# A gated transformer kernel on one core: the RWKV time mixing with 64-row products, an interleaved second tile level, centred values, and squares by token halves

## The reference, cut to what matters

```python
kk = kk / max(norm(kk), 1e-12)                     # heads of 64
k = k * (1 + (a - 1) * k_a)
# per head, state S (value x key), over tokens:
S_t = S_{t-1} diag(w_t) + (S_{t-1} a_t) b_t^T + v_t k_t^T ;  y_t = S_t r_t
mu = mean(y, over the head's 64); var = mean((y - mu)**2)
y = (y - mu) * rsqrt(var + GN_EPS) * gn_w + gn_b
y = y + sum(r * k * r_k) * v
return (y * g) @ w_o
```

## Time and profile before

| | us |
|---|---|
| median of 3 runs | 1428.78 |
| lowest and highest | 1426.89, 1428.99 |
| span of the profiled execution, first to last instruction | 1420.2 |
| PE busy | 1375.6 |
| DVE busy | 1049.1 |
| ACT busy | 733.2 |

### The profile page before, as it was taken

The page is one execution under the profiler, slowest core; times in us unless marked ns, Lnnn a source line. Parts: engine busy times, 40 slices in busy tenths (PEclk is TensorE's granted clock), DMA queues, the critical chain, the costliest instruction groups (busy, mean ns, idle before and its releaser), DMA issues.

```text
span 1420.2 us, 30753 instructions
## 1 busy us (share of the span) xinstructions
PE 1375.6 (97%) x11830; PEld 1310.7 (92%) x11830; DVE 1049.1 (74%) x1649; ACT 733.2 (52%) x1194; POOL 219.2 (15%) x232
## 2 busy tenths in 40 slices
PE   8999999999999999999999999999999999999997
PEld 6998899999988899999878888799999998999997
DVE  7988799987887889974787965777774556677743
ACT  4547555644556556664366442554444447544442
POOL 0000133310000223320000010113320000133300
PEclk9999999999999999999999999999999999999999
DMA  9874367797663547675322300346666433466661
GB/s 377 303 258 171 123 226 234 258 394 252 205 226 105 208 165 254 216 232 173 151 98 90 120 2 2 116 133 186 188 208 203 141 115 120 144 197 197 208 205 69
DMA packets 68434, 258.20 MB, mean 182 GB/s; under 512 B 7545, under 2 KB 9857, under 8 KB 67970
## 3 DMA queue, kind: packets, MB, share of 16 engines
q1 hardware_dynamic: 68354, 257.10, 54.2%
HBM read 256.01 MB, written 1.06 MB: 181 GB/s over the span
## 4 chain that ended last, share of the span: by engine, by line
PE 81%; DVE 11%; ACT 3%; issue 2%; DMA 2%; DVEq 0%; ACTq 0%
PE ps L740 21%; PE ps L742 20%; PE ps L741 20%; PE ps L757 3%; DVE lo L1919 2%; PE ps L701 2%; PE ps L703 1%; PE ps L702 1%; ACT hi L1370 1%; DMA modraw<-in_wmod 1%; DVE U L2508 1%; DMA modlast<-in_wmod 1%; DVE products L2506 1%; DVE modraw L1925 1%; PE ps L764 1%
## 5 line engine op out<-in xcount | busy, mean ns | idle before, releaser
L1919 DVE TENSOR_TENSOR lo<-raw,hi 128x1024 fp32r<-128x1024 f32 (+1 forms) x350 | 476.5, 1378 | 168.5 <-ACT hi L1370 167.8
L740 PE MATMUL ps<-OH,lo 128*128 128x256 f32 x1920 | 540.8, 282 | 6.2 <-DVE lo L1919 6.0
L742 PE MATMUL ps<-OH,hi 128*128 128x256 f32 x1920 | 534.8, 279 | 0.0
L741 PE MATMUL ps<-OL,hi 128*128 128x256 f32 x1920 | 534.8, 279 | 0.0
L1370 ACT ACTIVATE hi<-raw 128x1024 fp32r<-128x1024 f32 (+1 forms) x350 | 381.0, 1112 | 10.4 <-DMA raw<-in_w 6.1
L740 PEld LDWEIGHTS ps<-OH,lo 128*128 128x128 f32 x1920 | 362.0, 189 | 12.7 <-DVE lo L1919 9.9
L741 PEld LDWEIGHTS ps<-OL,hi 128*128 128x128 f32 x1920 | 362.4, 189 | 0.0
L742 PEld LDWEIGHTS ps<-OH,hi 128*128 128x128 f32 x1920 | 361.0, 188 | 0.0
L740 PE MATMUL ps<-GH,lo 128*128 128x256 f32 x704 | 196.3, 279 | 0.0
L742 PE MATMUL ps<-GH,hi 128*128 128x256 f32 x704 | 196.2, 279 | 0.0
L741 PE MATMUL ps<-GL,hi 128*128 128x256 f32 x704 | 196.2, 279 | 0.0
(11 more groups left out here) (389 smaller groups left out, 2059.5 us busy)
## 6 DMA issues: line engine op xcount, KB each, us to landing
raw<-in_w SPq DMA_DIRECT2D x288, 512.0 KB, 3.9
raw<-in_w SPq DMA_DIRECT2D x64, 704.0 KB, 5.3
modraw<-in_wmod SPq DMA_DIRECT2D x71, 512.0 KB, 5.2
modlate<-in_wmod SPq DMA_DIRECT2D x10, 512.0 KB, 4.0
modlast<-in_wmod SPq DMA_DIRECT2D x7, 512.0 KB, 4.5
modfirst_a<-in_wmod SPq DMA_DIRECT2D x4, 512.0 KB, 11.4
modfirst_b<-in_wmod SPq DMA_DIRECT2D x4, 512.0 KB, 12.1
l<-in_lora_in SPq DMA_DIRECT2D x1, 1536.0 KB, 6.2
```

Source lines behind the costliest of these rows:

```text
L740: pe.matmul(bank[:, 0:T], lo[:, r, w], oh[:, k0 + k], start=first, stop=False)
L741: pe.matmul(bank[:, 0:T], hi[:, r, w], ol[:, k0 + k], start=False, stop=False)
L742: ins = pe.matmul(bank[:, 0:T], hi[:, r, w], oh[:, k0 + k], start=False, stop=final)
L1919: dve.tensor_tensor(lo[:, s, 0:kt * P], raw[:, s, 0:kt * P], hi[:, s, 0:kt * P].bitcast(F32), ALU.subtract).then_inc(lo_made, 1)
```

## The change

It has four parts.

1. `z_part` and `u_part` do each product as two, one for tokens 0 to 63 and one for tokens 64 to 127 (`TOKEN_HALVES`), each with a stationary matrix of 128 x 64.
2. `second_level(x, t)` replaces `second_x` and `second_t`: the second tile's x products alternate with the first tile's t products, and the second tile's t products stand behind `z_part(0)`. ACT and DVE lists follow.
3. DVE makes `centre` = identity minus 1/64 within a head, over the place of the constant `bucket`. The 16 transposes of `V_` become ordinary float32 products with it, so that `VR` holds centred values. The four sums of `Yc` and the four subtractions are gone.
4. Squares go by `PAIRS` (tile, half of the channels): two of the four, and half of the sums, move ahead of `y_part(2)`. The table of the root is loaded earlier; the splits of two weight units stand before and behind the root.

```diff
         ident, ones, heads_ones = const("ident"), const("ones"), const("heads")
+        centre = const("bucket")
...
+        TOKEN_HALVES = slice(0, RN), slice(RN, P)
...
-                    ins = pe.transpose(PS[g % 4][:, q * P:(q + 1) * P], rw_src(g, q), ident)
+                    if g < 4:
+                        ins = pe.matmul(PS[g % 4][:, q * P:(q + 1) * P], rw_src(g, q), centre, start=True, stop=True)
+                    else:
+                        ins = pe.transpose(PS[g % 4][:, q * P:(q + 1) * P], rw_src(g, q), ident)
...
-            def second_x(tb):
-                pe.wait_ge(S("zeros_made"), 1)
-                pe.wait_ge(S("level_by_act"), 2 * tb + 5)
-                pe.wait_ge(S("level_by_dve"), tb + 3)
-                for n in range(RH * tb, RH * (tb + 1)):
-                    ins = pe.matmul(PS[2 * tb + (n % RH) // 8][RN:P, (n % 8) * RN:(n % 8 + 1) * RN], AT[0:RN, n, RN:P],
-                                    Tm[0:RN, n], start=True, stop=True)
-                ins.then_inc(S("level_done"), 1)
...
-            def second_t(tb):
-                pe.wait_ge(S("zeros_made"), 4)
...
-                for n in range(RH * tb, RH * (tb + 1)):
-                    ins = pe.matmul(PS[2 * tb + (n % RH) // 8][0:RN, (n % 8) * RN:(n % 8 + 1) * RN], X64[tb][RN:P, n % RH],
-                                    TT[RN:P, n, RN:P], start=True, stop=True)
-                ins.then_inc(S("level_done"), 1)
+            def second_x(n):
+                tb = n // RH
+                return pe.matmul(PS[2 * tb + (n % RH) // 8][RN:P, (n % 8) * RN:(n % 8 + 1) * RN], AT[0:RN, n, RN:P],
+                                 Tm[0:RN, n], start=True, stop=True)
...
+            def second_t(n):
...
+            def second_level(x, t):
+                if x is not None:
+                    pe.wait_ge(S("zeros_made"), 1)
+                    pe.wait_ge(S("level_by_act"), 2 * x + 5)
+                    pe.wait_ge(S("level_by_dve"), x + 3)
+                if t is not None:
+                    pe.wait_ge(S("zeros_made"), 4)
+                    pe.wait_ge(S("diag_placed"), 1)
+                    pe.wait_ge(S("level_by_act"), t + 8)
+                    pe.wait_ge(S("level_by_dve"), t + 6)
+                for n in range(RH):
+                    if x is not None:
+                        last_x = second_x(RH * x + n)
+                        if n == RH - 1:
+                            last_x.then_inc(S("level_done"), 1)
+                    if t is not None:
+                        last_t = second_t(RH * t + n)
+                        if n == RH - 1:
+                            last_t.then_inc(S("level_done"), 1)
...
-                        ins = pe.matmul(dst, apk[k % 2][:, b % 2, q, 0:P], v, start=True, stop=(tb == 0))
+                        for t in TOKEN_HALVES:
+                            ins = pe.matmul(dst[t], apk[k % 2][:, b % 2, q, t], v, start=True, stop=(tb == 0))
                         if tb:
-                            ins = pe.matmul(dst, AR[:, 4 * (b // 2) + q, 1, 0], SZ[:, head(b, q)], start=False, stop=True)
+                            for t in TOKEN_HALVES:
+                                ins = pe.matmul(dst[t], AR[:, 4 * (b // 2) + q, 1, 0, t], SZ[:, head(b, q)], start=False, stop=True)
...
-                        ins = pe.matmul(bank_of(k)[:, (4 * (b % 2) + q) * RN:(4 * (b % 2) + q + 1) * RN],
-                                        TT[:, RH * tb + 4 * b + q], Zs[k % 2][:, b % 2, q], start=True, stop=True)
+                        for t in TOKEN_HALVES:
+                            ins = pe.matmul(bank_of(k)[t, (4 * (b % 2) + q) * RN:(4 * (b % 2) + q + 1) * RN],
+                                            TT[:, RH * tb + 4 * b + q, t], Zs[k % 2][:, b % 2, q], start=True, stop=True)
...
-            second_x(0)
-            second_x(1)
+            second_level(0, None)
             pe.wait_ge(S("apb_made"), 2)
             half_gram(1)
-            second_t(0)
-            second_t(1)
+            second_level(1, 0)
             z_part(0)
+            second_level(None, 1)
...
+            def square_sums(k):
+                tb, g = PAIRS[k]
+                pe.wait_ge(S("gnsq_ready"), k + 1)
+                for c in range(2 * g, 2 * g + 4):
+                    ins = half_sums(PS[4][0:RH, tb * P:(tb + 1) * P], GQ[:, c, tb * P:(tb + 1) * P], c)
+                if k == 3:
+                    ins.then_inc(S("gnvar_done"), 1)
+            pe.wait_ge(S("bon_by_v"), 4)
+            square_sums(0)
+            square_sums(1)
             y_part(2)
             y_part(3)
-            pe.wait_ge(S("bon_by_v"), 4)
-            pe.wait_ge(S("yc_copied"), 4)
-            for g in range(4):
-                pe.matmul(PS[g][:, :], heads_ones, Yc[:, 2 * g:2 * g + 2].rearrange("p c t -> p (c t)"),
-                          start=True, stop=True).then_inc(S("gnsum_done"), 1)
-            for c in range(DC):
-                pe.wait_ge(S("gnsq_ready"), c // 2 + 1)
-                ins = half_sums(PS[4][0:RH, 0:T], GQ[:, c], c)
-            ins.then_inc(S("gnvar_done"), 1)
+            square_sums(2)
+            square_sums(3)
...
+            place_diagonal(3)
             for tb in range(2):
                 act.wait_ge(S("level_done"), tb + 5)
...
                 if tb == 0:
-                    place_diagonal(3)
-            place_diagonal(0)
-            place_diagonal(1)
+                    place_diagonal(0)
...
+            def square(k):
+                tb, g = PAIRS[k]
+                part = slice(2 * g, 2 * g + 4), slice(tb * P, (tb + 1) * P)
+                act.wait_ge(S("yc_copied"), k + 1)
+                act.activation(GQ[:, part[0], part[1]], Yc[:, part[0], part[1]], ACT.Square).then_inc(S("gnsq_ready"), 1)
+            square(0)
+            square(1)
+            act.preload_act_table(ACT.Sqrt)
             z_copy(3)
-            for copy in (u_copy, y_copy):
-                copy(2)
-                copy(3)
-            for r in range(LEAD, SLOTS):
-                weights_hi("rw_v", COUNT["rw_v"] // SLOTS - 1, r, KT)
-            act.preload_act_table(ACT.Sqrt)
-            for g in range(4):
-                act.wait_ge(S("gn_centred"), g + 1)
-                act.activation(GQ[:, 2 * g:2 * g + 2], Yc[:, 2 * g:2 * g + 2], ACT.Square).then_inc(S("gnsq_ready"), 1)
+            u_copy(2)
+            u_copy(3)
+            y_copy(2)
+            square(2)
+            y_copy(3)
+            square(3)
+            weights_hi("rw_v", COUNT["rw_v"] // SLOTS - 1, LEAD, KT)
             take_root(root[0:RH, 0], PS[4][0:RH, 0:T], 1 / RN, gn_eps[0:RH], S("gnvar_done"), 1, S("stage_root"))
+            weights_hi("rw_v", COUNT["rw_v"] // SLOTS - 1, LEAD + 1, KT)
...
+            chain.add(stt(out=centre, in0=heads_ones, scalar=-1 / RN, in1=ident, op0=ALU.mult, op1=ALU.add))
...
+            half_masks(1)
             second_x_out(1)
-            half_masks(1)
...
-            for g in range(4):
-                dve.wait_ge(S("gnsum_done"), g + 1)
-                y = Yc[:, 2 * g:2 * g + 2].rearrange("p c t -> p (c t)")
-                stt(out=y, in0=PS[g][:, :], scalar=-1 / RN, in1=y, op0=ALU.mult, op1=ALU.add).then_inc(S("gn_centred"), 1)
-            for r in range(LEAD, SLOTS):
-                weights_lo("rw_v", COUNT["rw_v"] // SLOTS - 1, r, KT)
             dve.wait_ge(S("g_scaled"), DC)
-            def by_gain(g):
-                dve.wait_ge(S("gnsq_ready"), g + 1)
-                chain.add(dve.tensor_tensor(Yc[:, 2 * g:2 * g + 2], Yc[:, 2 * g:2 * g + 2], G2[:, 2 * g:2 * g + 2], ALU.mult))
-            by_gain(0)
-            by_gain(1)
+            def by_gain(k):
+                tb, g = PAIRS[k]
+                part = slice(2 * g, 2 * g + 4), slice(tb * P, (tb + 1) * P)
+                dve.wait_ge(S("gnsq_ready"), k + 1)
+                chain.add(dve.tensor_tensor(Yc[:, part[0], part[1]], Yc[:, part[0], part[1]], G2[:, part[0], part[1]], ALU.mult))
+            for k in range(4):
+                by_gain(k)
+            weights_lo("rw_v", COUNT["rw_v"] // SLOTS - 1, LEAD, KT)
             dve.wait_ge(S("stage_root"), 5)
             dve.reciprocal(products[0:RH], root[0:RH, 0]).then_inc(S("gninv_ready"), 1)
-            by_gain(2)
-            by_gain(3)
+            weights_lo("rw_v", COUNT["rw_v"] // SLOTS - 1, LEAD + 1, KT)
```

More of the change, by code:

```diff
@@ L1181, in second_t @@
-            def second_t(tb):
-                pe.wait_ge(S("zeros_made"), 4)
-                pe.wait_ge(S("diag_placed"), 1)
-                pe.wait_ge(S("level_by_act"), tb + 8)
-                pe.wait_ge(S("level_by_dve"), tb + 6)
-                for n in range(RH * tb, RH * (tb + 1)):
-                    ins = pe.matmul(PS[2 * tb + (n % RH) // 8][0:RN, (n % 8) * RN:(n % 8 + 1) * RN], X64[tb][RN:P, n % RH],
-                                    TT[RN:P, n, RN:P], start=True, stop=True)
-                ins.then_inc(S("level_done"), 1)
+            def second_x(n):
+                tb = n // RH
```

(13 more changed lines are left out.)

## The result

The changed kernel takes 1418.21 us in the median of 15 runs (1405.74 to 1424.82), the kernel before 1427.5 us in 15 runs beside it (1420.04 to 1435.05). The ratio is 0.9944, with a 95% interval of 0.992 to 0.9968: 8.0 us less, between 4.6 and 11.4 (the two medians themselves lie 9.3 apart).

The account below looks back on a forecast made before the run. PE was taken as the bound, busy 1375.6 of 1420.2 us. 8.8 + 1.9 + 4.5 - 0.9 - 3.7 = 10.6 us less gave a span of 1409.6, plus 8.6 a median of 1418.2; range 1415.4 to 1422.6.

Parts of the forecast that it names:

- Halves: In `z_part` and `u_part`: 160 half products take 9.9 us where 80 whole ones took 18.7, 8.8 us less.
- Alternation: In the second level: sixteen pairs at opposite corners cost what sixteen single products do, 1.9 us less.
- Centring and squares: Sums of `Yc` and the wait before them go, 4.5 us less; ordinary products for the values start the level 0.9 later.
- The front: Ahead of the second level: dearer products for the values delay the filler, so `first_x` starts 0.9 us later, at 825.8.
- New waits: PE's waits in the stage for copies, masks, the last square and the reciprocal: 3.7 us more, bounds 2.5 and 5.5.
- The sum: Whole kernel: all gains less the later start and the added waits, 10.6 us less, a span of 1409.6 us.
- The step to the total: From profiled span to median of the runs: 8.6 us added to 1409.6, giving 1418.2 us.
- a sign against: PE's waits in the stage adding up to over 8 us, in place of about 5.5, would make the prediction wrong.
- halves in turn: Rival for z and u: halves run one after the other, 160 cost 19.3 us, total 1425.6; chance 0.08.
- a half at the price of a whole: Rival for z and u: each half costs as much as a whole, 160 cost 38 us, total 1444; chance 0.04.
- corners that don't overlap: Rival in the second level: alternating products gain nothing, 1.9 us more less 0.1 of waits, total 1420.0; chance 0.08.
- Masks that hold PE more: Rival: each of three mask waits grows by 0.6 and copy waits too, 3 us lost, total 1421.2; chance 0.10.

Follow-up runs that it names:

- e1: The kernel before with only the token halves of `z_part` and `u_part`; stage 73.35 us against 80.03, ratio to the kernel before 0.9929.
- e3: The changed kernel with the second level in its old order, not alternating; level and rest 53.90 us against 53.27, ratio to the kernel before 0.9931.
- e4: The kernel before with only the centred values and the squares changed; stage 77.11 us against 80.03, ratio to the kernel before 0.9981.
- e9: The changed kernel with eight filler passes for twelve ahead of `first_x`; `first_x` 8.47 us after the first product against 9.33, stage 69.61 us.
- e5: The changed kernel with masks made and waited for by bank, not all six at once; stage 67.47 us against 70.13, ratio to the kernel before 0.9891.

## Why the prediction was right, step by step

- **Halves.** 18.7 to 9.9 us was given. Measured: z 1.08 + 0.99 + 1.87 + 1.92, u 1.10 + 1.10 + 1.94, 10.0 in all. The form that `state_part` already had the earlier trace rows was the right row, and the shared moving operand is free. The rule of the Trainium skill's page "TensorE: Matmul & The Clock Gate" (Part 3), that a weight load overlaps running products only at another row group (though the same Part also names a background weight buffer as a way), does not hold here: both halves use all rows, and 64 records went through in 1.87 us with weight loads busy for all of it. Level and rest gained some 0.2 us more than z and u show (8.7 in e1, 18.5 less 10.0 here): the neighbours, which have the same form now, start sooner; `state_part(0)` took 0.95 (855.16 to 856.11) where it took 1.09.
- **Alternation.** 1.9 less products was right within 0.1 (838.61 to 840.71 for 64 records, a short wait in it). Its net worth is 0.6 (e3): the wait of 0.8 that I counted as new is its price, and it was 0.9.
- **Centring and squares.** 4.5 less and 0.9 more were given; 3.7 and 1.2 came out (e4). In the 3.7 are the last waits, 0.4 and 0.2, which the prediction counts as new waits. The sums of squares, taken as equal, are in two stretches now and some 0.3 dearer.
- **The front.** `first_x` at 825.8 was given, 825.95 came. It is the fixed filler that carries the delay on (e9).
- **New waits.** 3.7 in sum was given, 3.5 measured: 0.1 and 0.1 at the half gram and z, 0.9 at the copy, 0.7 and 1.1 at the masks where 0.8 and 0.8 stood, none ahead of `pair_gram(2)` (0.2 given), 0.4 at the square (0.6), 0.2 at the reciprocal (0.3): the spread starts 2.88 after the filler in front of it, and started 2.70 after it. PE's idle time in the stage is 5.3 us, where about 5.5 was expected and 8 would have been a sign against; the clock stayed at 1.00.
- **The sum.** 10.6 was given, the stage gave 9.9. The halves fell short by 0.3 (0.2 of it `z_part(3)`, which took 3.5 before and not 3.7, as I took from its like), the front by 0.3, the squares by 0.3; the waits were 0.2 shorter. The bounds as the prediction lists them add up to 1416.1 to 1421.6 and not to 1416.0 to 1421.3.
- **The step to the total** was not what I said. The 8.6 us between the profiled span and the median are no fixed cost. Each of those 61 runs of the kernel before took 2.1 to 2.2 us more than its span, and so did e1's; each run of a kernel with the centred values took 1.7 to 1.9 more (the first of the runs after: 1406.55 with a span of 1404.8). So 0.3 to 0.4 us of the gain lie outside the span, of which the forecast knew nothing, and the rest of the 8.6 is how far one execution, with its paces, lies from the median. That the forecast of 1418.2 met the median of 1418.21 so closely is luck: its gain of 10.6 was 0.7 too large for the stage and 2.6 too large by the ratio of the runs, and the median of the kernel before, from which it was taken, came down by 1.3 when more runs were made.

The rivals: halves in turn (1425.6) and a half at the price of a whole are excluded by 1.08 us for 32 records, and corners that don't overlap by 2.10 us for 64 records. Masks that hold PE more came true by 0.3 at one of three places.

## What to carry to other kernels

Where a stationary matrix is full and the moving side short, cut the stationary one into column halves: the row to price it by is any product of the same form already in the trace. Then ask at once which elementwise work the longer products covered; here 1.8 of 8.7 us went back at the masks, and e5 won it again by waiting for the banks in two groups instead of for all. Compare variants by a stage cut at fixed instructions, not by the total, when the total's executions differ by 20 us.

## What the runs showed of the hardware

- Uninterrupted products of 128 x 256 ran at 116 or at 112 ns, at the same granted clock, in different layers of one execution and in one layer of different executions. Over the two layers of glu0 it moved the total by some 7 us (a lead of 9.9 that grew to 16.6).
- The granted clock fell to 0.50 for some 13 us in one profiled execution of twelve, after small products with 1.19 us of idle time, and cost 5.7 us in the level; with 0.46 to 0.77 of idle time at the same place it stayed at 1.00.
- That idle time, named issue, was 0, 0.46, 0.47, 0.54, 0.77 or 1.19 us at nearly the same instructions.
- Products of 128 x 64 that write PSUM rows 0 to 63 and 64 to 127 in turn took 0.029 us a record (64 in 1.87), where whole ones of 128 x 128 with the same 64 moving columns took 0.12; 64 x 64 products at opposite corners of the array took 2.1 us for 64 records, where one corner alone took 3.87 for 64.
